# Expert weights in transfers of 2 MB, slots freed by halves, and first marks from the ranks, in a two-layer mixer and expert kernel

## The reference

```python
g_prob = softmax(xt @ w_rg + b_rg);  g_val, g_idx = top_k(g_prob, 1)
e_in_group = the four logits xt @ w_re + b_re of that group
e_val, e_loc = top_k(e_in_group, 2)
e_w = softmax(e_val) * g_val
for e in range(16):
    h = silu(xt @ w_gate[e]) * (xt @ w_up[e])
    out = out + combine[:, e:e + 1] * (h @ w_down[e])
```

## Time and profile before

| | |
|---|---|
| median of 3 runs | 1735.91 us (1733.82 to 1738.47) |
| profiled execution | 1732.53 us |
| its span | 1730.8 us |
| TensorE busy | 1568.8 us, 91% |
| VectorE busy | 926.5 us, 54% |
| ScalarE busy | 522.8 us, 30% |
| HBM read | 544.04 MB, 316 GB/s over the span |

### The profile page before, as it was taken

How to read it: one execution, slowest core, us unless ns; L and a number is a source line. 1 busy time by engine, 2 the same in 40 slices (tenths; PEclk the granted TensorE clock), 3 DMA queues, 4 the chain that set the end, 5 groups by cost and what they waited for, 6 DMA issues and landing times.

```text
span 1730.8 us, 35353 instructions
## 1 busy us (share of the span) xinstructions
PE 1568.8 (91%) x14820; PEld 1060.2 (61%) x14821; DVE 926.5 (54%) x1444; ACT 522.8 (30%) x602; POOL 48.4 (3%) x36
## 2 busy tenths in 40 slices
PE   8999999997999999966699999999989999986664
PEld 8999899885444444322299999998744444432221
DVE  7658655646555555431477476466475554552234
ACT  4552543423121212110264543533232112111011
POOL 0004000000000000000000040000000000000000
PEclk9999999999999999988899999999999999998887
DMA  9553455588999999999975544555999999999996
GB/s 305 202 179 126 160 167 189 195 337 351 420 422 422 418 419 400 424 421 422 410 235 180 162 144 160 166 191 195 392 373 421 421 422 422 419 423 422 422 421 269
DMA packets 139206, 547.28 MB, mean 316 GB/s; under 512 B 23060, under 2 KB 26360, under 8 KB 88568
## 3 DMA queue, kind: packets, MB, share of 16 engines
q1 hardware_dynamic: 138740, 546.13, 80.9%
q10 hardware_dynamic: 388, 0.04, 0.0%
HBM read 544.04 MB, written 2.10 MB: 316 GB/s over the span
## 4 chain that ended last, share of the span: by engine, by line
PE 74%; SPq 15%; DMA 4%; DVE 4%; issue 2%; DVEq 1%; ACT 0%; ACTq 0%
PE ps L808 24%; PE ps L1048 14%; PE ps L965 10%; SPq L432 9%; PE ps L1066 7%; SPq L436 5%; PE ps L805 5%; PE ps L1031 4%; PE ps L1012 3%; DMA room<-in_w_down_dram 3%; PE ps L1020 1%; DVE room L1118 1%; DVE h L1118 1%; PE ps L934 1%; PE ps L884 1%
## 5 line engine op out<-in xcount | busy, mean ns | idle before, releaser
L1048 PE MATMUL ps<-room 128*32 128x256 f32 x6016 | 371.2, 404 | 96.6 <-DMA room<-in_w_up_dram 91.1
L1118 DVE TENSOR_TENSOR w_lo<-room,w_hi 128x2048 fp32r<-128x2048 f32 (+1 forms) x121 | 281.4, 2335 | 232.9 <-ACT w_hi L520 232.4
L1048 PEld LDWEIGHTS ps<-room 128*32 128x32 f32 x6016 | 201.2, 116 | 282.0 <-DMA room<-in_w_up_dram 111.6
L808 PE MATMUL ps<-hT_hi,w_hi 128*128 128x256 f32 x1152 | 330.9, 287 | 0.9 <-DVE w_lo L1118 0.7
L808 PE MATMUL ps<-hT_hi,w_lo 128*128 128x256 f32 x1152 | 327.8, 285 | 0.0
L808 PE MATMUL ps<-hT_lo,w_hi 128*128 128x256 f32 x1152 | 327.7, 284 | 0.0
L520 ACT ACTIVATE w_hi<-room 128x2048 fp32r<-128x2048 f32 x120 | 228.3, 1914 | 228.4 <-PE ps L808 102.0
L1118 DVE TENSOR_TENSOR h<-h,ps 128x512 f32<-128x512 f32 x376 | 232.9, 681 | 98.0 <-PE ps L1031 97.5
L808 PEld LDWEIGHTS ps<-hT_hi,w_hi 128*128 128x128 f32 x1152 | 223.0, 194 | 3.8 <-issue 2.4
L808 PEld LDWEIGHTS ps<-hT_hi,w_lo 128*128 128x128 f32 x1152 | 223.0, 194 | 0.7 <-issue 0.5
L808 PEld LDWEIGHTS ps<-hT_lo,w_hi 128*128 128x128 f32 x1152 | 222.9, 194 | 0.0
(11 more groups left out here) (248 smaller groups left out, 1406.3 us busy)
## 6 DMA issues: line engine op xcount, KB each, us to landing
room<-in_w_gate_dram SPq DMA_DIRECT2D x128, 1024.0 KB, 19.0
room<-in_w_up_dram SPq DMA_DIRECT2D x128, 1024.0 KB, 21.0
room<-in_w_down_dram SPq DMA_DIRECT2D x128, 1024.0 KB, 16.5
room<-in_w_in_dram SPq DMA_DIRECT2D x88, 1024.0 KB, 5.0
room<-in_w_out_dram SPq DMA_DIRECT2D x32, 1024.0 KB, 5.0
room<-in_ln_g_dram SPq DMA_DIRECT2D x5, 1024.0 KB, 7.1
room<-in_ln_b_dram SPq DMA_DIRECT2D x5, 1024.0 KB, 9.0
h<-in_x_dram SPq DMA_DIRECT2D x4, 512.0 KB, 6.3
```

The costliest lines, as they stand in the source:

```text
L808: last = eng.matmul(ps[:, b + o // 2, (o % 2) * T:(o % 2) * T + T], w_[:, o * P:o * P + P], x_[:, kk, :], start=opens and o % 2 == 0, stop ...
L1048: last = eng.matmul(ps[r0:r0 + BLK, 0, 0:2 * P], xe[:, x0:x0 + BLK], unit_gu(u)[:, :, k, c * P:c * P + P], start=(i == 0 and k == 0), stop ...
L1118: return eng.tensor_tensor(o, a, b, op)
```

## The change

- `hot` of the first block is made from the ranks alone: expert 0's block 0 takes the tokens whose rank in expert 0 is the slot's number. The table for experts 0 and 1 needs no sorting either, as they come first. The sort, the positions and the weights follow after the first rows are taken.
- Gate and up are loaded as halves, a unit each (2 MB in one transfer, a run of 16 KB per partition, where a quarter had 8 KB); down's units are one transfer each as well. Two neighbouring slots make a pair, and one matmul reads gate and up out of both.
- `gu_half` takes the place of the three `gu_quarter`. A pair of units is waited for, and freed, together.
- `place` is no longer made from spread rows. VectorE multiplies the marks by the weights (`weigh`), TensorE turns them by eight matmuls in each block (`place_block`, after `scatter(g, 1)`), and ScalarE copies the result. The spreading matmuls, `rows`, and their copy are gone.
- The shift of the norm is no longer added by VectorE: it is loaded (8 KB) as four rows of `yraw`, and the first block's scatter adds it by a `place` of zeros and ones. The gain is multiplied as before, in two operations at other places, and is loaded behind the first nine units.
- ScalarE turns the first 128 tokens (`by_features(0)`) ahead of the router's copy.

```diff
@@ SP, in the loop over units
-                for m, v in enumerate((ln1_g, ln1_b)):
-                    eng.dma_start(gb[:, m, :], v[l:l + 1].to_broadcast([P, D])).then_inc(gb1_loaded.sem, 16)
...
+                    if u == SLOTS:
+                        eng.wait_ge(yraw_zero.sem, yraw_zero.at(l, 1))
+                        eng.dma_start(gain_1, ln1_g[l:l + 1].to_broadcast([P, D])).then_inc(gb1_loaded.sem, 16)
+
+                        eng.dma_start(yraw[0:P:BLK, :], ln1_b[l].rearrange("(c n) -> c n", c=4)).then_inc(gb1_loaded.sem, 16)
...
-                        eng.wait_ge((*gu_quarter, gu_done, y_half, y_done)[(u - SLOTS) % PER_E], last_block)
+                        eng.wait_ge((gu_half, gu_half, gu_done, gu_done, y_half, y_done)[(u - SLOTS) % PER_E], last_block)
...
-                        for m, w in enumerate((w_gate, w_up)):
-                            src = weights(w, e).rearrange("(p k) n -> p k n", k=KD)
-                            eng.dma_start(unit_gu(u)[:, m], src[:, 4 * i:4 * i + 4, :]).then_inc(unit_loaded[u % SLOTS], 16)
+                        w = w_gate if gate_first(u - i % 2) == (i % 2 == 0) else w_up
+                        src = weights(w, e).rearrange("(p k) n -> p k n", k=KD)
+                        eng.dma_start(unit_half(u), src[:, 8 * (i // 2):8 * (i // 2) + 8, :]
+                                      ).then_inc(unit_loaded[u % SLOTS], 16)
...
-                        for f in range(2):
-                            eng.dma_start(unit_down(u)[:, f, :], src[:, 2 * (i - 4) + f, :]
-                                          ).then_inc(unit_loaded[u % SLOTS], 16)
+                        eng.dma_start(unit_down(u), src[:, 2 * (i - 4):2 * (i - 4) + 2, :]
+                                      ).then_inc(unit_loaded[u % SLOTS], 16)
@@ TensorE, in and before expert_block
+                def place_block(g):
+
+                    eng.wait_ge(weighed_ready, g + 1)
+                    for t in range(NT):
+                        for c in range(4):
+                            r0 = BLK * c
+                            last = eng.matmul(ps[r0:r0 + BLK, 1, P + t * P:P + t * P + P], weighed[:, t, :], ident[:],
+                                              start=True, stop=True, tile_position=(0, r0))
+                    last.then_inc(place_done, 1)
...
-                    for i in range(4):
-                        u = first_unit + i
+                    for i in range(2):
+                        u = first_unit + 2 * i
                         loaded(u)
-                        for k in range(4):
-                            x0 = (4 * k + i) * BLK
+                        loaded(u + 1)
+                        for k in range(8):
+                            kk = 8 * i + k
+                            x0 = (4 * (kk % 4) + kk // 4) * BLK
...
-                        if i < 3:
-                            last.then_inc(gu_quarter[i], 1)
+                        if i == 0:
+                            last.then_inc(gu_half, 1)
...
                             scatter(g, 1)
+                            place_block(g)
@@ VectorE, after the ranks
+                counts = ps[:, 1, 0:NT * 16].rearrange("p (t e) -> p t e", t=NT)
+                tt(hot, iota[:].rearrange("p (o s) -> p o s", o=1).to_broadcast([P, NT, BLK]),
+                   counts[:, :, 0:1].to_broadcast([P, NT, BLK]), ALU.is_equal)
+                eng.drain()
+                tt(hot, hot, M[:, 2, :, 0:1].to_broadcast([P, NT, BLK]), ALU.mult).then_inc(first_hot.sem, 1)
...
+                def weigh():
+
+                    slots(place_iota)
+                    eng.drain()
+                    tt(hot_2[:], hot_2[:], wts.to_broadcast([P, 2, NT, BLK]), ALU.mult)
+                    ts(place_iota, place_iota, float(BLK), None, ALU.add)
+                    eng.drain()
+                    tt(weighed, hot_2[:, 0], hot_2[:, 1], ALU.add).then_inc(weighed_ready, 1)
...
+                ts(place, slot_of[:].to_broadcast([P, T]), 0.0, None, ALU.is_equal).then_inc(place_ready, 1)
...
-                tt(h[:, 0, :], h[:, 0, :], gb[:, 1, :], ALU.add)
-                tt(h[:, 1, :], h[:, 1, :], gb[:, 1, :], ALU.add)
-                eng.drain()
                 with eng.Fori(0, nb - 1) as j:
                     g = g0 + j
+                    weigh()
                     add_block(g, 0)
                     take_rows(xT_done, g + 1)
                     add_block(g, 1)
-                    place_rows()
-                    mark(hot_ready)
+                    mark()
```

More of the change, by code:

```diff
@@ L151, in trunk @@
         xrow, xe, yraw = area(64, 512), area(85, 512), area(48, 512)
-        place, place_2 = area(50, T), area(51, T)
-        place_l, place_l2 = area(56, T), area(57, T)
-        rows = area(52, 4 * T).rearrange("p (r t) -> p r t", r=4)
+        place = area(50, T)
+        weighed = area(51, NT * BLK).rearrange("p (t s) -> p t s", t=NT)
         wide = area(74, D)
@@ L301, in trunk @@
             semaphore(n) for n in ("y_done", "y_ready", "place_ready", "sc_done", "added"))
-        gu_quarter, y_half = [semaphore(f"gu_quarter_{i}") for i in range(3)], semaphore("y_half")
+        gu_half, y_half = semaphore("gu_half"), semaphore("y_half")
         block = ctx.enter_context(nc.Block())
@@ L702, in _ @@
                     half_evac(0, b)
+                by_features(0)
                 logits_evac(0)
@@ L707, in _ @@
                 logits_evac(1)
-                for t in range(NT):
-                    eng.activation(h_k[:, t], h[:, t, :].rearrange("a (p k) -> a k p", k=KD), ACT.Copy
-                                   ).then_inc(hk_ready.sem, 1)
+                by_features(1)
                 eng.wait_ge(ex_in.sem, ex_in.at(l, 1))
@@ L1078, in _ @@
                 turn_rows(first_rows.sem, first_rows.at(l, 1), first_turned.sem)
-                eng.wait_ge(wts_ready.sem, wts_ready.at(l, 1))
-                for i in range(2):
-                    for j, col in ((0, pos12), (1, wts)):
-                        for t in range(NT):
-                            last = eng.matmul(banks(4, 2)[:, (2 * j + i) * T + t * P:(2 * j + i) * T + t * P + P],
-                                              col[:, i, t, :].to_broadcast([P, P]), ident[:], start=True, stop=True)
-                last.then_inc(spread_done.sem, 1)
                 def expert(e, first_unit, period):
@@ L1516, in _, with take_rows @@
                                          ).then_inc(tab_first.sem, 1)
+                tt(sorted_by, key.rearrange("p (o n) -> p o n", o=1).to_broadcast([P, 16, 16]),
+                   key.rearrange("p (e o) -> p e o", o=1).to_broadcast([P, 16, 16]), ALU.is_gt)
+                eng.drain()
+                tt(sorted_blocks, sorted_by, tab[:, 0:1, :].to_broadcast([P, 16, 16]), ALU.mult)
+                eng.drain()
+                def take_rows(done, count):
+                    g_, b_ = (lnc[:, 2 * l + 1, i, :].rearrange("p (c q o) -> p q c o", q=4, o=1).to_broadcast([P, 4, 4, BLK])
+                              for i in range(2))
+                    x4 = xe.rearrange("p (q c s) -> p q c s", q=4, c=4)
+                    eng.wait_ge(done, count)
+                    tt(x4, ps[:, 3, :].rearrange("p (q c s) -> p q c s", q=4, c=4), g_, ALU.mult)
+                    eng.drain()
+                    tt(x4, x4, b_, ALU.add).then_inc(xe_ready, 1)
@@ new lines, in _ @@
+                take_rows(first_turned.sem, first_turned.at(l, 1))
+                eng.tensor_reduce(tab[:, 1, :], sorted_blocks, AX.X, ALU.add)
+                eng.drain()
+                eng.scalar_tensor_tensor(pos, tab[:, 1:2, :].to_broadcast([P, NT, 16]), float(BLK), counts, ALU.mult, ALU.add)
+                ts(block_iota, iota[:], float(BLK), None, ALU.add)
+                eng.tensor_copy(place_iota, iota[:])
+                eng.drain()
+                tt(t32[:], M[:, 0:2], pos.rearrange("p (o t) e -> p o t e", o=1).to_broadcast([P, 2, NT, 16]), ALU.mult)
@@ new lines, in _, with slots, mark @@
+                ts(tab[:, 1, :], tab[:, 1, :], carry[:], None, ALU.add)
+                eng.drain()
+                eng.tensor_reduce(pos12, t32[:], AX.X, ALU.add)
+                eng.drain()
+                def slots(iota_):
+                    return tt(hot_2[:], iota_.rearrange("p (o u s) -> p o u s", o=1, u=1).to_broadcast([P, 2, NT, BLK]),
+                              pos12.to_broadcast([P, 2, NT, BLK]), ALU.is_equal)
+                def mark():
+                    slots(block_iota)
+                    eng.drain()
+                    tt(hot, hot_2[:, 0], hot_2[:, 1], ALU.add).then_inc(hot_ready, 1)
+                    ts(block_iota, block_iota, float(BLK), None, ALU.add)
+                    eng.drain()
@@ L1526, in _ @@
                 eng.drain()
[L1527 to L1537 removed]
+                tt(wts[:, 1], wts[:, 0], ex[:, :, 4:5], ALU.mult)
                 def add_block(g, t):
```

122 lines of the change are left out of this document (45 added, 77 removed).

## The result

| | before | change |
|---|---|---|
| median | 1736.37 us (1730.5 to 1739.45, 10 runs) | 1747.97 us (1740.9 to 1749.74, 10 runs) |
| profiled execution, its span | 1732.5, 1730.8 us | 1740.9, 1739.1 us |
| ratio | | 1.0058, 95% interval 1.0045 to 1.0071 |

The change costs about 10 us (1736.37 x 0.0058; interval 7.8 to 12.3) where I had forecast 2.5, and it is slower by more than the 0.3% that can be told.

The account below looks back on a forecast made before the run. Taken as bound by the transfer stream, held up a little by late slots, with stream and slots tied. Terms 0.0 + 0.9 + 5.0 - 3.4 = +2.5 us gave 1735.0 us profiled, 1738.4 median; range 1731 to 1747.

Parts of the forecast that it names:

- Where the end is set: Two-block experts: slots freed by blocks, not the transfer stream, decide; 0.0 us in layer 0, +0.9 us in layer 1.
- Part 1: First block of each layer: marks from ranks alone and no spreading matmuls start block 0 3.85 us earlier.
- Part 2: Slots by halves: SP's tenth unit issued at 415.8, 2.1 us earlier; moved gain load and removed shift load worth 0.
- Part 3: Way to the first two-block expert: block 2 6.3 us earlier in layer 0, 4.8 in layer 1; 1.3 added for low clock.
- Part 4: Eight place matmuls lengthen every block by 0.30 us (bounds 0 and 0.45): 4.5 us in layer 0, 3.9 in layer 1.
- Slots: Sum at the two-block experts' slots: block 17 at 685.9 in layer 0; change 0.0 there, +0.9 us in layer 1.
- Part 5: Tail of each layer: the half behind the last landing takes 5.5 us, costing +2.5 us a layer, +5.0.
- Part 6: Gate and up transfers in 16 KB runs reach 428 GB/s, 0.074 us less a unit behind the last stall, -3.4 us.
- The other rule: Trainium skill's transfer-size rule: 1 MB gives 341 GB/s, 16 MB 425, so doubling transfers would gain far more than 3.4 us.
- Cost per transfer: Rival on weight loads: fixed cost per transfer, so down gains too, saving 5.4 instead of 3.4 us: 1736.4; chance 0.12.
- Packets give nothing: Rival on weight loads: larger packets bring no gain, the rest as summed, +5.9 us, 1741.8; chance 0.13.
- The slower rival: Tail half at 1.2 GHz throughout, 7.1 us, 4.1 a tail, and no packet gain: +9.1 us, 1745.0; chance 0.27.

Follow-up runs that it names:

- Experiment 1: The change with each of the eight place matmuls of a block issued twice: 1764.33 us, ratio 1.0152 to the kernel before.
- experiment 7: The change with gate and up in quarters (1 MB transfers, waited for and freed by quarters) and down in two transfers a unit: 1743.15 us, ratio 1.0036.
- Experiment 10: The change with VectorE's two gain products and the wait for the gain's load moved behind the sorted table: 1751.09 us, ratio 1.0082.
- Experiment 5: The kernel before with TensorE waiting for both quarters of a half before beginning it, loading and freeing unchanged: 1744.17 us, ratio 1.0043.
- experiment 3: The change with two full 128 x 128 turns in place of the eight place matmuls of each block: 1748.72 us, ratio 1.0059.
- experiment 8: The change with every unit loaded by two transfers of 1 MB, waiting and freeing by halves kept: 1752.14 us, ratio 1.0087.
- experiment 11: The change with gate and up by quarters, gain products behind the table, and place by two full turns: 1735.78 us, ratio 1.0003.
- experiment 6: The kernel before with slots of gate and up freed by halves and units awaited by halves: 1744.64 us, ratio 1.0042.

## Why the prediction was off

**Where the end is set: right.** Slots decided in both layers, the stream had slack, and the head start alone brought nothing at the end. Experiment 1 shows it: 0.44 us more in each block came back as 16 us of the total.

**Part 1, the earlier first block: right, but for the clock.** -4.8 and -3.2 us against -3.85 each. In layer 0, 1.3 of the 4.8 are a difference between two executions: the sixteen turns ahead of the router took 3.34 us before, at a granted clock of 0.58 from 396 to 400 us, and 2.07 in the change.

```profile
396.49 3.34 PE L934 MATMUL ps<-ident,h 128*128 128x128 f32 x16 [2.19 <-DVE h L1121]
```

```profile
396.38 2.07 PE L948 MATMUL ps<-ident,h 128*128 128x128 f32 x16 [1.77 <-DVE h L1140]
```

In layer 1 they took 2.07 in both. That leaves -3.5 and -3.2.

The forecast also took the spreading matmuls away as pure gain. They had kept TensorE at work until block 0; without them it idles 1.63 to 1.75 us just ahead of it. Block 0's gate and up product then took 8.63 to 8.80 us in 11 of the 18 first blocks (two layers each) of the change and its eight variants; it took 7.11 or 7.12 in all ten of the kernel before and its variants. One of the slow ones, in layer 1 of experiment 7:

```profile
1271.29 8.80 PE L1072 MATMUL ps<-room 128*32 128x256 f32 x128 [1.63 <-DVE room L1136]
```

The change's profiled execution had none, so it was spared 1.5 to 1.7 us a layer that others paid. No run fills the gap with work, so that the gap is the cause is argued; why 7 of the 18 stayed fast isn't known.

**Part 2: unit 9 right, the gain load wrong.** Unit 9 was issued at 414.81, 3.71 us behind block 0 (3.75 forecast). "Worth 0" for the gain load looked only at what stands behind it in the queue. Ahead of it stand the first nine units; gain and shift are awaited together, and the shift, issued at 401.49, landed only 14.3 us later:

```profile
401.49 0.62 SPq L422 DMA_DIRECT2D room<-in_ln_b_dram  x1
414.81 0.34 SPq L445 DMA_DIRECT2D room<-in_w_gate_dram  x1
```

VectorE waits 1.66 and 2.56 us for them, with the table queued behind that wait. Experiment 10 takes the wait out.

**Part 3: too small, and close in layer 0 partly by luck.** Block 2 came 38.3 us behind block 0 in layer 0 and 40.6 in layer 1, against 36.95 forecast for both: 1.4 and 3.7 too little. VectorE's first additions began 14.5 and 15.7 us behind block 0, 14.7 forecast. Since 1.66 and 2.56 of these were the wait of part 2, VectorE's own work had been put 1.9 and 1.6 us too high, and in layer 0 the two errors cancelled. What was too small is the low clock behind TensorE's gap (2.76 and 3.88 us). From the second scatter's start to block 1 the change takes 7.17 us in layer 0 and 8.06 in layer 1, where 1284 to 1293 us have a granted clock of 0.52, near 1.2 GHz. In experiment 10, where TensorE didn't idle ahead of it, it takes 4.54 (block 1 at 432.63):

```profile
428.09 2.14 PE L1045 MATMUL ps<-room 32*128 32x512 f32 x8
```

So the low clock cost 2.6 and 3.5 us there, and I had added 1.3.

**Part 4, the mis-sized term that grows with the blocks.** "32 of them in 1.08 us at 392.42" are 16 matmuls: the router's code issues 16 a call, and rows of this kind show two for one, as eight place matmuls show x16. Nor is a row's length what its matmuls take from TensorE: it ends with the last one's own 0.27 us. Eight make a row of 0.65 us and sixteen one of 1.08, so eight more cost 0.43, or 0.054 each. With the right count alone the term would have been 0.54 and further off, on the other side. Measured are 0.47 from start to start, 0.43 in the period inside an expert, 0.34 across a border, 0.40 on the mean, against 0.30. Over 15 and 13 blocks that is 1.5 and 1.1 us. The upper bound, 0.45, held the period.

**Slots.** Block 17 began 276.7 us behind block 0 and not 273.85 (the 1.4 of part 3 and the 1.5 of part 4); in layer 1 block 15 246.8 and not 241.95. Of these 2.9 and 4.8 us, 2.0 and 3.9 reached the last landing; 0.9 came back in the single-block experts. Less than a microsecond is noise in such a split: the last two landings of layer 1 are 10.74 us apart, where the other such pairs of the change are 9.70 to 9.80.

**Part 5: right in kind, 0.7 short a layer.** From the last gate or up landing to the norm the time rose by 3.2 us in either layer (14.00 to 17.23 and 13.75 to 16.98). The half took 6.3 to 6.4 us and not 5.5, at a granted clock of 0.61 and 0.63, and the place matmuls are in it. Down's wait was gone, as forecast. Experiment 5 has the cost by itself.

**Part 6: right.** With 16 KB runs two units took 9.7 to 9.8 us, and 4.194 MB / 9.8 = 428 GB/s is the estimate. A single-block expert takes 29.52 us instead of 29.84, 0.08 for each gate or up unit (0.074 forecast). The first two-block experts ran at 425, but there the faster stream only lengthens the stall.

**The other rule.** The Trainium skill (DMA: Bandwidth & Descriptors, Bandwidth) has larger transfers much faster, measured with transfers that GpSimd issues. Here SyncE issues them. By this case's rows the transfer's size changes nothing (29.83 against 29.84 us for six units), and the run's size 1.4% (428 against 422). So the measurements decide against it here, where transfers are queued back to back.

**Rivals and sum.** "Cost per transfer" fell. "Packets give nothing" fell. The slower rival came near the time, 1745.0, but not for its reason: its half at 1.2 GHz throughout (7.1 us) would have added 4.1 a layer, 3.2 were measured, and its packet loss didn't happen. The missing 5.8 us between +2.5 and +8.3 are 2.7 and 4.6 in the stages, less 1.5 outside them. On the median shown of 1735.91 the ratio makes 1746.0 us (1743.7 to 1748.2), at the upper edge of the range of 1731 to 1747; the median of the ten runs is 1.0 us above it. The likeliest outcome, a time within 0.3%, was wrong. I gave it because terms of a few microseconds cancelled, and three that I sized from a row or two were too small: the low clock behind the gap (part 3), the place matmuls (part 4) and the half behind the last landing (part 5). The path that I had named was the right one apart from the gain's wait; these sizes were not. That the time fell inside the range is owed to the width that the slower rival gave it, not to the sum.

**Left open.** Why the median of the change lies 7 us above its profiled execution while that of before lies 4 above its own. Two slow first blocks would make 3.4 us of it, and the four variants whose profile shows two (experiments 3, 7, 8 and 11) lie within 1.2 us of their own medians; but no profile shows a slower execution of the change itself. Whether halves of slots and of waits overlap (experiment 6). What makes block 0 slow in some executions and not in others.

## What to carry to other kernels

Count issued instructions in the code, not in the trace's rows, and take a price from the difference of two rows, since a row's length holds the last instruction's own time. A term of 0.30 us instead of 0.40, multiplied by 28 blocks, made 2.7 of the 7.3 us that the two expert stages took beyond the forecast. A head start is worth what the next resource can follow: price it together with the transfer stream behind it, since the same reordering cost 4 us with halves and gained 8 with quarters. Matmuls that a change removes may have filled a gap ahead of a long product: look at what that product takes afterwards, in several executions. Where TensorE waits for weights, the piece behind the last landing is paid in full, and at a lower clock than the steady state's.

## What the chip showed unexpectedly

- Size of a run, not of a transfer, sets the rate of queued loads: 387 GB/s for 2 KB (w_in, from 12 to 22 us), 422 for 8 KB, 428 for 16 KB per partition.
- Two turns of 128 by 128 took 0.36 us where eight column-group matmuls took 0.47, and what they saved came back as a gap of 0.29 us at TensorE's own queue between experts.
- The 128 gate and up matmuls of block 0 took 8.80 us in one layer and 7.11 in the other of the same execution (experiment 10), after waits of 1.75 and 1.74 us. Over all profiles it was 8.63 to 8.80 us in 11 of 18 cases behind such a wait, and in none of 10 without one.
